# Sample recurrence of a hybrid decoder step: the four state scalings moved from one GpSimd multiplication each to eight ScalarE copies each

## The reference, cut to what matters

```python
f = lb + (1.0 - lb) * jax.nn.sigmoid(rf)          # forget gate, one number per state row
k = 1.0 - f
S_new = f[:, None] * S + k[:, None] * i[None, :]   # per sample and head, S is (REC_DK, REC_DV)
o = q @ S_new
```

## Time and profile before

| | |
|---|---|
| runs | 1236.65, 1237.36, 1240.8 us; median 1237.36 |
| the profiled execution | 1245.5 us, of which the span is 1243.7 us |
| mean granted clock of PE | 0.987 |
| busy in the span | PE 1208.1 us, DVE 880.3, ACT 486.1, POOL 228.2 |

### The profile page before, as it was taken

How to read it: one execution, slowest core, us unless ns; L and a number is a source line. 1 busy time by engine, 2 the same in 40 slices (tenths; PEclk the granted TensorE clock), 3 DMA queues, 4 the chain that set the end, 5 groups by cost and what they waited for, 6 DMA issues and landing times.

```text
span 1243.7 us, 23606 instructions
## 1 busy us (share of the span) xinstructions
PE 1208.1 (97%) x9397; PEld 1192.9 (96%) x9397; DVE 880.3 (71%) x1525; ACT 486.1 (39%) x997; POOL 228.2 (18%) x162
## 2 busy tenths in 40 slices
PE   9799999999999999999999999999999999999997
PEld 8799999999999999999999999999999999999996
DVE  4767657574646765789877788878888575567676
ACT  5544453634222155455422232222223235455542
POOL 1000010100101000000023346557655220000011
PEclk9999999999899899999999999999999999999999
DMA  8412110104345324324344456677686367686466
GB/s 286 119 34 74 35 35 1 37 18 67 56 66 74 104 86 145 112 69 128 102 146 146 153 183 217 221 252 214 218 249 205 129 203 216 202 259 185 146 153 117
DMA packets 174014, 169.82 MB, mean 137 GB/s; under 512 B 23144, under 2 KB 126328, under 8 KB 173376
## 3 DMA queue, kind: packets, MB, share of 16 engines
q1 hardware_dynamic: 171728, 164.78, 45.2%
q0 software_dynamic: 2176, 3.52, 1.8%
HBM read 116.73 MB, written 52.58 MB: 136 GB/s over the span
## 4 chain that ended last, share of the span: by engine, by line
PE 60%; DVE 5%; issue 1%; ACT 0%; DVEq 0%; ACTq 0%
PE pair L1806 33%; PE pair L1846 18%; PE pair L1765 6%; PE pair L1546 3%; DVE mix L2285 1%; DVE mix L2310 1%; DVE w_lo L2243 1%; DVE qinv L2281 1%; PE pair L1737 0%; PE pair L1748 0%; DVE act_lo L2293 0%; PE pair L1678 0%; DVE mix L2448 0%; DVE acc L2347 0%; DVE mix L2268 0%
## 5 line engine op out<-in xcount | busy, mean ns | idle before, releaser
L1806 PE MATMUL pair<-act_hi,w_hi 128*128 128x258 f32 x704 | 199.6, 284 | 4.3 <-DVE w_lo L2243 2.7
L1806 PE MATMUL pair<-act_hi,w_lo 128*128 128x258 f32 x704 | 198.9, 283 | 0.0
L1806 PE MATMUL pair<-act_lo,w_hi 128*128 128x258 f32 x704 | 198.8, 282 | 0.0
L1846 PE MATMUL pair<-a_ring,w_hi 128*128 128x258 f32 x1056 | 189.7, 283 | 0.6 <-DVE mix L2448 0.4
L1546 PE MATMUL pair<-act_hi,w_hi 128*128 128x344 f32 x528 | 179.9, 341 | 5.0 <-DVE act_lo L1924 4.1
L1546 PE MATMUL pair<-act_hi,w_lo 128*128 128x344 f32 x528 | 171.5, 325 | 0.0
L1546 PE MATMUL pair<-act_lo,w_hi 128*128 128x344 f32 x528 | 171.3, 324 | 0.0
L1846 PEld LDWEIGHTS pair<-a_ring,w_hi 128*128 128x128 f32 x1056 | 162.6, 189 | 1.6 <-DVE mix L2448 0.9
L1806 PE MATMUL pair<-s_hi,w_lo 128*128 128x258 f32 x528 | 149.3, 283 | 0.0
L1806 PE MATMUL pair<-s_hi,w_hi 128*128 128x258 f32 x528 | 149.2, 283 | 0.0
L1806 PE MATMUL pair<-mix_r,w_hi 128*128 128x258 f32 x528 | 149.0, 282 | 0.0
(11 more groups left out here) (323 smaller groups left out, 2647.4 us busy)
## 6 DMA issues: line engine op xcount, KB each, us to landing
raw<-w_up_dram SPq DMA_DIRECT2D x26, 512.0 KB, 5.2
a_in<-h_sums SPq DMA_DIRECT2D x44, 258.0 KB, 3.4
rawx<-w_gate_dram SPq DMA_DIRECT2D x22, 512.0 KB, 4.9
w_quarter<-w_down_dram SPq DMA_DIRECT2D x44, 256.0 KB, 3.9
w_sums<-w_quarter SPq DMA_DIRECT2D x44, 256.0 KB, 4.5
rawx<-w_sums SPq DMA_DIRECT2D x44, 256.0 KB, 3.9
raw<-w_in_dram SPq DMA_DIRECT2D x18, 512.0 KB
h_scratch<-mix SPq DMA_DIRECT2D x23, 258.0 KB, 2.1
```

The lines of the kernel that those rows point to most:

```text
L1806: mm = pe.matmul(pair[psum_pair(n)][:, s, 0:QW], a[:, r, half + k, :], b, start=(k == 0 and i == 0), stop=(k == 3 and i == 2))
L1846: mm = pe.matmul(dpair(mt)[:, s, 0:a.shape[1]], b[:, cut], a, start=(m == 0 and n == 0), stop=(m == HALVES - 1 and n == 2))
```

## The change

The multiplication on POOL goes. In its place ACT scales the state of each sample by its own gate column, with eight ACTIVATEs of 128 x 128 whose scale is a pointer to `f_s`. They stand one tick later in ACT's list than POOL's did in POOL's, at ticks 100, 106, 112 and 118. DVE's eight additions get a name of their own (`r_sum`) and stay at their tick. The semaphore waits are the same.

```diff
@@ sample_steps @@
         for h in range(NREC):
             d = tick - (SR0 + SRS * h)
-            out += [(s, h) for s, v in (("r_scale", 0), ("r_outer", 2), ("r_o", 4)) if d == v]
+            out += [(s, h) for s, v in (("r_scale", 0), ("r_outer", 1), ("r_sum", 2), ("r_o", 4)) if d == v]
@@ GpSimd @@
-                if step[0] == "r_scale":
-                    h = step[1]
-                    pool.wait_ge(sem("st_in"), 16 * (h + 1))
-                    pool.wait_ge(sem("f_done"), h + 1)
-                    pool.tensor_tensor(st[:], st[:], bc(f_s[:, h, :].unsqueeze(2), [P, DECB, P]), ALU.mult).then_inc(sem("st_scaled"), 1)
@@ ScalarE @@
+                if step[0] == "r_outer":
+                    h = step[1]
+                    act.wait_ge(sem("st_in"), 16 * (h + 1))
+                    act.wait_ge(sem("f_done"), h + 1)
+                    for b in range(DECB):
+                        ins = act.activation(st[:, b, :], st[:, b, :], ACT.Copy, scale=f_s[:, h, b:b + 1])
+                    ins.then_inc(sem("st_scaled"), 1)
@@ VectorE @@
-                if step[0] == "r_outer":
+                if step[0] == "r_sum":
                     h = step[1]
                     dve.wait_ge(sem("s_ib"), 16 * (h + 1))
                     dve.wait_ge(sem("st_scaled"), h + 1)
```

## The result

The changed kernel is slower. The median of 5 runs is 1247.79 us (1246.1 to 1249.16) against 1240.39 us (1236.65 to 1243.28) for 5 runs of the kernel before; the ratio is 1.0075, 95% interval 1.0055 to 1.0095, which is 9.3 us of 1240. The forecast was 1235.9.

What follows compares the result with a forecast made beforehand. PE was taken as the bound, busy 1208.1 of 1243.7 us, so other engines' work counts only where PE waits or its clock falls. Terms -5.0 - 3.4 + 6.9 = -1.5 us, laid on the median, gave 1235.9 us, range 1229.5 to 1241.5.

Steps and rivals of the forecast that it cites:

- The chain at B: Near 381 us: copies (2.4 us), DVE's additions, gate read, `f_s`, then `hk` 3.6 us later; PE waits 3.9 us.
- B: Near 381 us, sample head 1: copies ahead of `hk` of prompt head 3; +3.6 wait, +3.3 half clock, +6.9 us.
- place A: Near 328 us: DVE no longer stopped by POOL, wait 2.41 to 0.7 us, following half clock gone; -5.0 us.
- place C: Near 400 us: wait 2.17 to 0.5 us (-1.7), another -1.7 up to level 5; -3.4 us.
- The clock term of B: Behind PE's wait for `hk` near 381 us: one added half-clock stretch of 6.8 us, costing +3.3 us.
- The stretch at 413.4: Half clock for 6.8 us from 413.4 us, expected to stay because a wait before level 5 precedes it.
- The wait before level 5: Near 411 us: DVE can't follow PE, so PE waits some 2.4 us in place of 0.78.
- the timed runs have less of something: Median 8.1 us below the profiled execution, perhaps fewer half-clock stretches, which would make gains and loss smaller.
- B takes over: Rival, chance 0.21: slower through PE's wait for `hk` at 381 us, copies near 3.9 us; +4.1 us, 1241.5 us.

Runs made afterwards that it cites:

- Experiment 1: Changed kernel with the state of sample head 1 scaled by GpSimd again, heads 0, 2 and 3 on ScalarE; ratio to before 0.9983.
- Experiment 2: Changed kernel with only head 1 scaled by ScalarE, GpSimd scaling heads 0, 2 and 3 as before; ratio to before 1.0101.
- kernel 10: Changed kernel with head 1's copies two ticks later, behind `hk`, its additions and sample products moved back too; ratio to before 0.9982.
- Experiments 7: Kernel before, GpSimd's multiplication of heads 0 and 2 held until VectorE starts `hq` and `hk`, forcing a collision; ratio to before 1.0033.
- kernel 8: Kernel before, GpSimd's multiplication of heads 0 and 2 held until VectorE has finished `hk` of level 1; ratio to before 0.9983.
- experiments 6: Changed kernel with GpSimd scaling head 1 and VectorE's additions of head 2 one tick later; median 1235.12 us, ratio to before 0.9976.
- 9: Kernel before with GpSimd held for heads 0 and 2 until `hk` of level 1, and head 2's additions one tick later; ratio 0.9993.

## Why the prediction was wrong

- *The chain at B* was right to 0.2 us: copies 2.44 us (2.4), wait 4.05 (3.9), read and gate behind the additions. Experiments 1, 2 and 10 show that B is the whole loss.
- *Between the two profiled executions* most terms came as worked out. Taking each wait's beginning from the lines above and the earlier trace rows, PE came from place A to its need of `hk` 4.7 us sooner (forecast 5.0), and through place C to level 5 3.3 us sooner (3.4). From `hk` to level 3 it took 9.3 us longer (6.9). Behind level 5 1.4 us were lost (0), and 0.1 ahead of place A. The sum is +2.8 where -1.5 was forecast for this pair; the rest of the miss lies in carrying the pair over to the median.
- *The clock term of B, +3.3 us, was mis-sized.* It was one stretch of 6.8 us. The two profiles of the changed kernel show 13.7 and 17.1 us, in which PE worked for 11.9 and 16.4; that is 5.8 and 8.0 us by the earlier trace rows. With 3.7 us more of waiting this makes 9.5 to 11.7. The price of B in the runs is 11 to 13 us, and 6.9 was forecast.
- *Place A, -5.0, and place C, -3.4, are the step that failed.* Their events were read rightly (DVE stopped, 2.41 to 0.68 us, 2.17 to 0.47), but they were taken to be in every execution. "By chance" stood in the text, and the sum charged both in full to the median. Experiment 1 shows what A and C give in the runs: 2.1 us (0.4 to 3.8), where 8.4 was forecast. Experiment 2's profile shows GpSimd missing `hk` at both places. Experiments 7 and 8 have the price, 6.2 us between two forced collisions and a kernel that mostly avoids them, so the executions of before have about a third of it on average, as an estimate. That they draw it anew each time is argued from this and from the spread; it was not seen in two profiles of the kernel before.
- *The stretch at 413.4* was kept with its 6.8 us; it had 10.2 in the changed profile and 6.8 in its second. The wait before level 5 came as worked out (2.4; 2.32).
- *The hint that was there:* the profiled execution stood 8.1 us over the median, and the text said that "the timed runs have less of something". It then laid the whole sum on the median. With the 29 runs of before on one chip, the mean granted clock goes from 0.995 at 1234.6 us to 0.986 at 1243.9: the spread goes with half-clock time, and the profile was from its upper end. The collisions are not all of that spread. The 11 runs of kernel 10, where GpSimd scales nothing, still lie between 1235.3 and 1241.7. Near 50 us, far from the change, 8 of the 13 profiles have 3.4 us of half clock and 5 have 10.2, which is 3.3 us. The base was low as well: 1237.36 from 3 runs, where 29 runs gave 1240.0. With A and C at -2 and B at its forecast +6.9 the sum would have been +5, slower.
- *The rival "B takes over"* had the right place and sign. It was given 0.21, with its price hung on dear copies; the copies were as cheap as expected and the clock made the price.
- *The skill's rule.* The Trainium skill, "GPSIMD Engine Reference", section "Key points", says that GpSimd contends with VectorE instructions that have two SBUF inputs. The traces agree: 0.69 to 2.43 us with two such inputs, 1.30 and 0.52 undisturbed with one. Taken up, it would have said that a collision needs such an instruction at that moment.

What stays open: why the later additions of head 2 gave nothing in experiments 6 and 9, how often GpSimd meets `hk` in the executions of before, and how much of the 2.1 us at A and C is waiting and how much clock.

## What to carry to other kernels

Ahead of moving work to an idle engine, look at what stands next in that engine's queue and who waits for it: here the copies were cheap, hidden for three heads of four, and cost 1% for the one head where they stood ahead of `hk`. A wait on TensorE is to be priced with the clock behind it: at `hk` the half clock cost 5.8 to 8.0 us and the wait 3.7 more than before. An event in one profile that hangs on a DMA's landing is a draw: when the profiled execution is well off the median, price such events at less than full, or look at a second execution.

## What was not expected of the hardware

- Filling a wait of 4 us on TensorE with 24 matmuls that no one needs made the kernel 10 to 11 us faster.
- Half clock came without a long wait as well: in experiment 2, with 0.71 us of waiting at place A, two stretches of 3.4 us stood near 328 and 335 us, where few-column products and 344-column ones alternate. In six other profiles the same place with the same wait (0.69 to 0.71 us) had none.
- GpSimd's multiplication and a VectorE instruction with two SBUF tensors exclude each other: the later of the two stands until the other's end (2.43 us for 0.69), and GpSimd takes longer than its 1.90 us when it comes second (2.13 us before, 2.28 in kernel 8).
